# C's value products: turned probabilities and values split in halves and multiplied in float32r

## The reference, cut to what matters

```python
s = jnp.einsum("nqhgd,nkhd->nhgqk", q, k).astype(jnp.float32) * scale
s = jnp.where(mask[:, None, None], s, NEG)          # chunk-causal, chunks of 64
p = jax.nn.softmax(s, axis=-1)
return jnp.einsum("nhgqk,nkhd->nqhgd", p.astype(v.dtype), v)
```

## Time and profile before

| | us |
|---|---|
| median of 3 runs (lowest, highest) | 3233.89 (3228.85, 3236.66) |
| the profiled execution | 3230.68 |
| its span, from first to last instruction | 3228.9 |
| PE busy in the span | 2901.2 (90%) |
| DVE busy | 1787.8 (55%) |
| ACT busy | 1196.9 (37%) |
| C's attention block, first scores to last output, layer 0 | 610.49 to 698.17 |
| the same, layer 1 | 2201.15 to 2288.82 |

### The profile page before, as it was taken

The page is one execution under the profiler, slowest core; times in us unless marked ns, Lnnn a source line. Parts: engine busy times, 40 slices in busy tenths (PEclk is TensorE's granted clock), DMA queues, the critical chain, the costliest instruction groups (busy, mean ns, idle before and its releaser), DMA issues. The chain is left out here.

```text
span 3228.9 us, 49051 instructions
## 1 busy us (share of the span) xinstructions
PE 2901.2 (90%) x19080; PEld 2738.2 (85%) x19080; DVE 1787.8 (55%) x2845; ACT 1196.9 (37%) x2477; POOL 140.3 (4%) x254
## 2 busy tenths in 40 slices
PE   4888879889899999999968888788789999999997
PEld 2787778679899999999947868677789999999997
DVE  5366764643655555554654587465436555545554
ACT  5555644642322212122245565456423222212222
POOL 0200012000000000000002000120000000000000
PEclk8996989889999999999979969898999999999999
DMA  4110001031111111111031100110411111111111
GB/s 178 32 57 30 23 26 41 10 123 45 53 46 46 46 47 40 47 51 42 20 125 47 48 23 21 33 35 11 151 34 46 50 43 46 40 53 46 40 46 62
DMA packets 182277, 161.76 MB, mean 50 GB/s; under 512 B 14488, under 2 KB 169880, under 8 KB 181528
## 3 DMA queue, kind: packets, MB, share of 16 engines
q1 hardware_dynamic: 182040, 158.45, 15.6%
HBM read 129.56 MB, written 29.06 MB: 49 GB/s over the span
## 5 line engine op out<-in xcount | busy, mean ns | idle before, releaser
L1798 PE MATMUL ps<-h_hi,w_hi 128*128 128x352 f32 x2496 | 547.8, 328 | 49.1 <-DVE w_lo L1909 23.0
L1798 PE MATMUL ps<-h_hi,w_lo 128*128 128x352 f32 x2496 | 542.0, 324 | 8.2 <-issue 8.2
L1798 PE MATMUL ps<-h_lo,w_hi 128*128 128x352 f32 x2496 | 540.9, 325 | 0.0
L1798 PEld LDWEIGHTS ps<-h_hi,w_hi 128*128 128x128 f32 x2496 | 427.5, 191 | 65.5 <-issue 44.7
L1798 PEld LDWEIGHTS ps<-h_hi,w_lo 128*128 128x128 f32 x2496 | 431.3, 189 | 0.0
L1798 PEld LDWEIGHTS ps<-h_lo,w_hi 128*128 128x128 f32 x2496 | 427.5, 189 | 0.0
L2249 ACT ACTIVATE cv<-up,cols 128x1058 f32<-128x1058 f32 x88 | 112.0, 1273 | 735.0 <-issue 695.0
L785 PE MATMUL ps<-w_hi,h_hi 128*128 128x256 f32 (+1 forms) x1152 | 335.3, 291 | 24.1 <-DVE w_lo L962 18.2
L786 PE MATMUL ps<-w_lo,h_hi 128*128 128x256 f32 (+1 forms) x1152 | 329.5, 286 | 0.0
L787 PE MATMUL ps<-w_hi,h_lo 128*128 128x256 f32 (+1 forms) x1152 | 327.4, 284 | 0.0
L2360 DVE TENSOR_TENSOR x_t<-ps,x_t 128x1056 f32<-128x1056 f32 x176 | 221.0, 1256 | 159.3 <-PE ps L1798 158.6
(11 more groups left out here) (214 smaller groups left out, 4232.6 us busy)
## 6 DMA issues: line engine op xcount, KB each, us to landing
stage<-in_f_win SPq DMA_DIRECT2D x88, 512.0 KB, 3.8
stage<-in_f_wout SPq DMA_DIRECT2D x44, 512.0 KB, 3.7
stage<-in_w_in SPq DMA_DIRECT2D x40, 256.0 KB, 4.2
x_spill<-x_t SPq DMA_DIRECT2D x2, 4224.0 KB, 13.8
x_t<-x_spill SPq DMA_DIRECT2D x2, 4224.0 KB
stage<-in_w_o SPq DMA_DIRECT2D x16, 512.0 KB, 4.5
w_raw<-in_w_in SPq DMA_DIRECT2D x24, 256.0 KB, 4.0
o_in<-o_spill SPq DMA_DIRECT2D x8, 528.0 KB, 6.9
```

Source lines behind the costliest of these rows:

```text
L1798: last = pe.matmul(ps[:, s0 + b, 0:BAND], lh, rh_[:, b * BAND:(b + 1) * BAND], start=(first_k and n == 0), stop=(last_k and n == 2))
```

## The change

`attention_c` passes a new region to the stage (`pair`), and with it steps 6 to 8 change, in C alone. The copy on ACT rounds the turned probabilities to float32r (`pt`). A new DVE step, `turned_low`, subtracts that from the PSUM bank and keeps the rest in `pt_lo`. The values are split in the same way, once for each tile of keys: ACT rounds (`high_values`), DVE subtracts (`low_values`), and both halves of a head lie side by side in `v_pair` (64 + 64 columns). For each segment PE then issues one product of `pt` with both halves (128 columns) and one of `pt_lo` with the high half (64 columns, added to the first 64). The output takes two DVE instructions, the second of which waits for the first. PE's waits on `pt_copied` become waits on `pt_low`.

```diff
         prob = (prob_at or w).take("prob", [P, 4, 1024])
-        pt = (pt_at or w).take("pt", [P, 2, 9, P])
+        pt = (pt_at or w).take("pt", [P, 2, 9, P], F32R if pair else F32)
+        if pair:
+            pt_lo = pair.take("pt_lo", [P, 2, 9, P], F32R)
+            v_pair = pair.take("v_pair", [P, 13, 4, P], F32R)
+            part = pair.take("part", [P, 4, 64])
...
+            elif pair:
+                if p >= 4:
+                    eng.wait_ge(S.o_copied, p - 3)
+                eng.tensor_scalar(part[0:r, p % 4, :], ps[0:r, 6 + p % 2, 64:P], scale, None, ALU.mult).then_inc(S.out_part, 1)
+                eng.wait_ge(S.out_part, p + 1)
+                eng.scalar_tensor_tensor(to, src, scale, part[0:r, p % 4, :], ALU.mult, ALU.add).then_inc(S.o_copied, 1)
...
-                            pe.wait_ge(S.pt_copied, g - 1)
+                            pe.wait_ge(S.pt_low if pair else S.pt_copied, g - 1)
...
-                    pe.wait_ge(S.pt_copied, first_group[p + 1])
+                    pe.wait_ge(S.pt_low if pair else S.pt_copied, first_group[p + 1])
...
+                    if pair:
+                        pe.wait_ge(S.v_low, v_sum[j + 1])
+                        vh = jobs[j]["v_head"]
+                        both, high = ps[0:r, 6 + p % 2, 0:P], ps[0:r, 6 + p % 2, 0:64]
+                        for n, (_, kt, _, kn) in enumerate(sg):
+                            pe.matmul(both, pt[0:kn, p % 2, n, 0:r], v_pair[0:kn, kt, vh, :], start=(n == 0), stop=False)
+                            last = pe.matmul(high, pt_lo[0:kn, p % 2, n, 0:r], v_pair[0:kn, kt, vh, 0:64],
+                                             start=False, stop=(n == len(sg) - 1))
...
+                def turned_low(p):
...
+                    for n, grp in enumerate(turn_groups(p)):
+                        g = first_group[p] + n
+                        dve.wait_ge(S.pt_copied, g + 1)
...
+                        dve.tensor_tensor(pt_lo[0:kn, p % 2, own, 0:r],
+                                          ps[0:kn, 4 + g % 2, 0:len(grp) * P].rearrange("p (m c) -> p m c", c=P)[:, :, 0:r],
+                                          pt[0:kn, p % 2, own, 0:r].bitcast(F32), ALU.subtract).then_inc(S.pt_low, 1)
...
                     divide(j)
+                    if pair:
+                        low_values(j)
+                        if j >= 1:
+                            turned_low(j - 1)
...
                 for j in range(NJ + 1):
+                    if pair and j < NJ:
+                        high_values(j)
                     if j + 1 < NJ:
                         exponent(j + 1)
...
-                               Region(R_W2 + 17408, R_END), tok=256)
+                               Region(R_W2 + 17408, R_END), tok=256, pair=Region(R_H, R_X))
```

More of the change, by code:

```diff
@@ L200, in build_program @@
         pt_copied = sem("pt_copied")
+        pt_low = sem("pt_low")
+        v_high = sem("v_high")
+        v_low = sem("v_low")
+        out_part = sem("out_part")
         pv_done = sem("pv_done")
@@ L1151, in attention_stage, with v_rows @@
     def attention_stage(jobs, v_of, products, nk, w, prob_at=None, pt_at=None, sinks=False, diff=False, tok=None, tiles=range(TILES),
-                        nxt=None, at=3):
+                        nxt=None, at=3, pair=None):
         prob = (prob_at or w).take("prob", [P, 4, 1024])
-        pt = (pt_at or w).take("pt", [P, 2, 9, P])
+        pt = (pt_at or w).take("pt", [P, 2, 9, P], F32R if pair else F32)
[3 more added lines that the diff above has]
+            part = pair.take("part", [P, 4, 64])
+            v_tiles = []
+            for jb in jobs:
+                own = [jb["tile0"] + c for c in range((jb["keys"] + P - 1) // P)]
+                v_tiles.append([kt for kt in own if not any(kt in x for x in v_tiles)])
+            v_sum = [sum(len(x) for x in v_tiles[:j]) for j in range(len(jobs) + 1)]
+        def v_rows(kt):
+            return DEC if kt == 12 else P
         mx = w.take("mx", [P, 4])
@@ L1289, in values @@
                     sg = segs(j)
+                    if pair:
[6 more added lines that the diff above has]
+                                             start=False, stop=(n == len(sg) - 1))
+                        last.then_inc(S.pv_done, 1)
+                        return
                     if one_head:
@@ L1383, in divide, with low_values @@
                     dve.scalar_tensor_tensor(second, second, rden[0:r, q % 4, 2:3], first, ALU.mult, ALU.add).then_inc(S.p_ready, 1)
+                def low_values(j):
+                    for n, kt in enumerate(v_tiles[j]):
+                        k = v_rows(kt)
+                        dve.wait_ge(S.v_high, v_sum[j] + n + 1)
+                        dve.tensor_tensor(v_pair[0:k, kt, :, 64:P], v_of(kt)[0:k, :].rearrange("p (h c) -> p h c", c=64),
+                                          v_pair[0:k, kt, :, 0:64].bitcast(F32), ALU.subtract).then_inc(S.v_low, 1)
+                def turned_low(p):
+                    r = jobs[p]["rows"]
+                    sg = segs(p)
+                    for n, grp in enumerate(turn_groups(p)):
+                        g = first_group[p] + n
+                        dve.wait_ge(S.pt_copied, g + 1)
+                        kn = sg[grp[0]][3]
+                        own = slice(grp[0], grp[0] + len(grp))
+                        dve.tensor_tensor(pt_lo[0:kn, p % 2, own, 0:r],
+                                          ps[0:kn, 4 + g % 2, 0:len(grp) * P].rearrange("p (m c) -> p m c", c=P)[:, :, 0:r],
+                                          pt[0:kn, p % 2, own, 0:r].bitcast(F32), ALU.subtract).then_inc(S.pt_low, 1)
                 def out_copy(p):
@@ L1412, in vector @@
                         nxt.hooks["low"](dve, j - at)
+                if pair:
+                    turned_low(NJ - 1)
                 for q in range(max(0, NPV - 3), NPV):
@@ L1458, in turned_copy, with high_values @@
                                  ).then_inc(S.pt_copied, 1)
+                def high_values(j):
+                    for kt in v_tiles[j]:
+                        k = v_rows(kt)
+                        act.copy(v_pair[0:k, kt, :, 0:64], v_of(kt)[0:k, :].rearrange("p (h c) -> p h c", c=64)).then_inc(S.v_high, 1)
                 exponent(0)
```

## The result

| | before | after |
|---|---|---|
| median, us (lowest, highest) | 3233.13 (3228.85, 3236.66) | 3331.94 (3324.32, 3333.46) |
| ratio, 95% interval | | 1.0297 [1.0275, 1.0318] |
| the profiled execution, us | 3230.68 | 3332.2 |
| C's attention block, us, each of the two layers | 87.7 | 137.7 |

The change made the kernel 3% slower. Both blocks of C together are 100 us longer, of 101.5 in the profiled executions; the stretches before, between and behind them changed by 4.4 us at most. The page of the kernel after shows where the clock went down: its digits for C's block are the 6 in the eighth and ninth slice and, for the second layer, the 5 and 7 in the twenty-eighth and twenty-ninth (before: 8 and 8, 8 and 9).

The account below looks back on a forecast made before the run. PE alone sets C's pace before, the ring of DVE and ACT after: 6.5 + 20.8 + 0.6 - 0.9 = 27 us a layer, 54 for both, on 3230.68 gives 3284.7, with 3.2 for the median 3288; range 3268 to 3314.

Parts of the forecast that it names:

- the ring: C's closed chain of copy, subtraction, output, maximum, exponential across ACT and DVE: 4.91 us at 1024 keys, loss 20.8 a layer.
- the clock: In C's long tiles, one or two short falls to half clock, 5 to 20 us; nothing in the sum.
- the samples' value tiles: Five value tiles in C come at once on DVE, 0.35 us each, and overrun the wait by about 0.6 us.
- the terms: Times of C's steps by segments and keys: subtractions 0.64 to 1.84 us, outputs 0.55, maximum with exponential 1.45 to 2.52.
- The short jobs: C's start up to job 15, where DVE's own time decides: loss 6.5 us a layer, 0.9 of it from half clock.
- The tail: C's end, from the maximum of job 35 to the last output: 6.0 us instead of 6.9, a gain of 0.9.
- PE's products: Each segment's two float32r products in C save PE 0 to 9 us in all; taken as nothing.
- the rival that was written down: The clock falls in C's long tiles because PE waits in each ring; at worst 27 us a layer, 3342; chance 0.15.
- the two stretches of B: B's attention: PE busy 4.67 of 6.80 us, then half clock; 45.52 of 55.60 kept it; C's fifth tile supposedly between.
- ceiling of 27 us a layer: C's 16 long prompt turns at half clock: 96 us of PE against 68 by the ring, 27 more a layer at worst.
- DVE's work hides: DVE's added 20 us in C fit into its 31 us of idle time after 633; about 3240; chance 0.04.
- faster: PE still ends last in every turn of C and the 64-column product saves 9 us: 3225; chance 0.03.

Follow-up runs that it names:

- e4: Changed kernel with the low part's product 128 columns wide instead of 64; one execution, 3297.45 us.
- e3: Changed kernel with DVE's maximum two jobs ahead everywhere instead of only among the short jobs; one execution, 3305.12 us.
- e8: Changed kernel with DVE's maximum two jobs ahead everywhere and both products of a segment 128 columns wide; 3261.38 us, 1.0116.
- e7: Changed kernel with 16 added float32r products of 512 columns at the head of PE's queue in C; 3286.18 us, 1.0167.
- e2: Changed kernel without DVE's subtractions of the turned probabilities, PE waiting for ACT's copy, low part set to zero once; one execution, 3264.16 us.
- e6: Changed kernel with PE's old float32 products, all ACT and DVE work and waits kept; timed over several executions, 3309.85 us, 1.0242.
- e10: Changed kernel with the pairs, subtractions and second output only for jobs 16 to 35, short jobs as before the change; 3307.36 us, 1.0217.
- e13: Changed kernel with pairs only from job 16 on, and the low part's product 128 columns wide; 3279.22 us, 1.0142.
- e15: Changed kernel with pairs only from job 16 on, 128 and 64 columns, and DVE's maximum one job further ahead; 3244.25 us, 1.0035.
- e14: Changed kernel with pairs only from job 16 on, DVE's maximum one job further ahead, and both products 128 columns wide; 3244.31 us, 1.0042.
- e1: Changed kernel with PE's old float32 products, all ACT and DVE work and waits kept; one execution, 3312.81 us.
- e5: Changed kernel with both products of a segment 128 columns wide, timed over several executions; 3310.44 us, 1.0217.
- e11: Changed kernel with 16 added products at C's start, DVE's maximum two jobs ahead everywhere, and both products 128 columns wide; 3253.68 us, 1.0043.
- e12: Changed kernel with 16 added products at C's start and both products of a segment 128 columns wide; 3293.91 us, 1.0177.

## Why the prediction was wrong

Forecast 3288, range 3268 to 3314, measured 3331.94. The direction and the ring were right, the clock was not: the sum put that term at nothing.

1. *The ring* (20.8 us a layer, and 0.6 for the samples' value tiles). Right: e4 shows 22.9 for both. Its turns are 4.78 to 4.99 us at 1024 keys (forecast 4.91) and 3.60 to 3.87 at 640 (forecast 3.6 to 3.9); e3 and e8, which open the ring, bring them back to 3.73. What is over lies in the first turn at 640 keys (4.43, by the terms 3.58) and the one that ends at the first sample job (4.75, by the terms 3.84). In both, new value tiles pass through the ring; the sum has a term for the samples' alone.
2. *The short jobs* (6.5). The maxima of jobs 0 and 15 of e4 are 26.7 us apart, 18.4 before: 8.3. The prices of the parts were right: start to start, DVE's part of a value tile took 0.34 (forecast 0.35), a low part of 512 columns 0.61 (0.605) and one of 384 0.46 (0.48). In e7, with the clock full before the first scores, the same distance is 22.4. So of the 8.3 us, 4.0 came with DVE's work alone (forecast 5.6), and 4.3 with the half clock at the start, 21 us in e4 (forecast 0.9, where 3 or 4 turns at 2.2 instead of 1.75 us would already have made 1.4 to 1.8).
3. *The tail* (a gain of 0.9). In e4 it grew by 1.3, from 6.9 to 8.2 us. Its clock was low there, from 718.8 on.
4. *PE's products* ("I take nothing"). Right, e2's second layer. At half clock the pair takes twice the time, as the float32 product does.
5. *The clock.* This is the step that failed: "But PE without gaps gets its clock back, as in C's start, so I expect one or two short falls, 5 to 20 us", with a chance of 0.15 for more than 10 and nothing in the sum. The one start that I had looked at came back after 13.7 us; nothing in the trace of before said that this holds for another mix of products. PE without gaps stayed at 0.50 for 78 us of the first two windows after. This is also not the rival that was written down: there waits of the ring were to lose a clock that had come, while here it had not come at all when the ring's tiles began, and PE did not wait. A reading of the rows was wrong as well: at 640 keys PE is at work for 2.33 of 3.7 us, 0.63, and that does not lie between the two stretches of B, 0.69 (the clock fell next) and 0.82 (it stayed), but below both. Without that a block is 120.3 to 120.7 (e4, e6), with it 137.7: 17 us a layer, 34 for both, with the longer low stretch in the sample tile (24.5 us against 10 in e4). The prediction's ceiling of 27 us a layer, worked out from PE's turns at half clock, was the right kind of estimate. The range gave it half its price, from a chance that was too small. (Its lower end, 3268, does not follow from the stated bounds, which give 3274.)

Together: 54 forecast, 11 for points 1 to 3 (32.6 instead of 27 a layer), 34 for the clock, 99 of the 101.5 between the profiled executions.

The rivals "DVE's work hides" and "faster" are out: at full clock the turns are the ring's in every kernel that has it. In the changed kernel's ring there were short falls too, of 3.4 us each (699.1 and 712.7), but they cost little.

*What stays open.* That e10's long fall needs the narrow products and the idle time is shown by e10, e13, e15 and e14. Why other falls in the same ring last 3 to 10 us is not, nor why the clock comes late at the block's start. The same instructions had it after 13.7 or 23.9 us or after 61 to 75 in different layers or executions (e1, e2, e4 and e5), with float32 products too (e1, e15), and after the warm start it fell for 47.8 us in one layer and not in the other (e11, e12). The changed kernel had it after 81.9 us in all four profiled blocks, and its times suggest the same for all its executions. Whether narrow products make a late clock likelier in the short jobs is suggested by this and by the times of e5 and e6, and not shown. In every profiled block of every version the clock is also low at the block's end, for the last 2 to 25 us (in e10 from long before), where before the change it fell some 1.6 us behind it; no run was made to find out why. No version beat the kernel before; the best, pairs for the long jobs with the ring opened (e14, e15), is 0.4% slower. e14's blocks are 5.7 us longer than before, with the clock low in the last 11; this was not taken apart.

## What to carry to other kernels

A step added to an in-order queue between two steps that wait on another engine can close a ring; add its links up and compare the sum with the pace of the bounding engine, whatever the busy shares say, and look for one iteration of slack to give to one of the links. Where PE's pace is near the edge, work out the price of half clock for the stretch and give it real weight: what one stretch of the trace shows on getting the clock back need not hold for other instructions, nor for the same ones in the next layer. Compare prices like with like: a duration is not the distance from start to start. Read the granted clock before explaining any difference of times, and compare both layers of one execution: in e2 the same instructions took 117.5 us in one and 87.8 in the other.

## What the chip showed that I had not expected

- PE without idle time can stay at 1.2 GHz long: 38.00 us busy of 38.00 (after), 67.50 of 67.50 (e10), 67.20 of 67.20 (e15). Before, it came back at the end of a low stretch of 13.7 us, PE being busy for all of its last 10.8 us.
- A float32r product of 128 columns and one of 64 take 0.14 and 0.08 us at full clock, 0.25 and 0.18 at half clock, together the same as a float32 product of 64 columns in its two passes (0.22 and 0.43).
- Widening the second product to 128 columns costs PE nothing here: a pair takes 0.11 + 0.11 us, the same 0.22. It saved 28 us in the ring (e13 against e10), since it kept the clock. PE was idle for 16% of the two windows shown of e13.
- Sixteen added products of 512 columns had the clock up 4.3 us after the first of them (e7), against 10.8 us into the block before and 79 in the changed kernel, and paid for themselves; the clock was not kept for good by it (e11, e12).
